# State-space rounds: 32-row matmuls for the decays and the head spread, and a skip term written by ScalarE

## The reference, cut to what matters

```
dt    = softplus(dt_raw + dt_bias)             # one per token, head and direction
y_fwd = ssd_chunked(x * dt_f, dt_f * A[0], B, C)
y_bwd = flip(ssd_chunked(flip(x * dt_b), flip(dt_b * A[1]), flip(B), flip(C)))
y     = y_fwd + y_bwd + ssd_D[:, None] * x     # the last is the skip term
ssd   = rms_norm(y * silu(z), ssd_norm_w)
# inside a chunk of 128 tokens, per head:
M[l, s] = (C[l] . B[s]) * exp(cs[l] - cs[s])  for s <= l    # cs: cumulative sum of dt * A
```

## Time and profile before

| | |
|---|---|
| median of 3 runs | 925.79 us |
| the three runs | 925.61, 925.79, 929.63 us |
| the profiled execution | 920.72 us |
| its span | 918.9 us |
| TensorE busy (page) | 894.4 us, 97% of the span |
| VectorE, ScalarE, GpSimd busy | 668.6, 512.5 and 79.0 us |
| mean granted TensorE clock | 0.994 |

### The profile page before, as it was taken

How to read it: one execution, slowest core, us unless ns; L and a number is a source line. 1 busy time by engine, 2 the same in 40 slices (tenths; PEclk the granted TensorE clock), 3 DMA queues, 4 the chain that set the end, 5 groups by cost and what they waited for, 6 DMA issues and landing times.

```text
span 918.9 us, 18092 instructions
## 1 busy us (share of the span) xinstructions
PE 894.4 (97%) x7444; PEld 851.2 (93%) x7444; DVE 668.6 (73%) x918; ACT 512.5 (56%) x696; POOL 79.0 (9%) x56
## 2 busy tenths in 40 slices
PE   5999999999999999999999999999998999999998
PEld 3899998888888889999999999988998999999998
DVE  6877998998699988777866545545886766666642
ACT  2566756577878774335555543446567654554431
POOL 0133000000455440000000000000000000000000
PEclk9999999999999999997999999999999999999999
DMA  9764553757322237483755655544431345555660
GB/s 377 305 244 147 198 190 121 280 217 251 116 90 93 92 131 260 184 302 118 283 191 183 206 206 184 183 155 167 139 138 47 138 144 200 206 184 183 231 205 23
DMA packets 25084, 168.00 MB, mean 183 GB/s; under 512 B 2868, under 2 KB 4532, under 8 KB 5048
## 3 DMA queue, kind: packets, MB, share of 16 engines
q1 hardware_dynamic: 23760, 164.90, 50.7%
q10 hardware_dynamic: 1256, 2.12, 0.7%
HBM read 165.95 MB, written 1.06 MB: 182 GB/s over the span
## 4 chain that ended last, share of the span: by engine, by line
PE 75%; DVE 10%; ACT 7%; DMA 4%; issue 3%; SPq 0%; DVEq 0%; ACTq 0%
PE bank L1864 74%; DVE wlo L1107 3%; ACT whi L573 3%; DMA raw<-w_stream 2%; DVE acc L1152 1%; DMA adas<-w_stream 1%; DVE cvt L1341 1%; ACT kw__113 L822 1%; PE bank L2137 1%; DVE eb L1432 1%; ACT ew L789 0%; DVE p L1319 0%; ACT prob L724 0%; PE bank L2161 0%; DVE kw__113 L1441 0%
## 5 line engine op out<-in xcount | busy, mean ns | idle before, releaser
L1864 PE MATMUL bank<-hhi,whi 128*128 128x256 f32 (+1 forms) x1364 | 382.8, 283 | 0.9 <-DVE hlo L1210 0.6
L1864 PE MATMUL bank<-hlo,whi 128*128 128x256 f32 (+1 forms) x1352 | 375.4, 278 | 0.0
L1864 PE MATMUL bank<-hhi,wlo 128*128 128x256 f32 (+1 forms) x1352 | 373.7, 278 | 0.0
L1107 DVE TENSOR_TENSOR wlo<-raw,whi 128x2048 fp32r<-128x2048 f32 (+1 forms) x130 | 298.9, 2300 | 101.0 <-ACT whi L573 98.9
L573 ACT ACTIVATE whi<-raw 128x2048 fp32r<-128x2048 f32 (+1 forms) x132 | 250.9, 1901 | 97.2 <-PE bank L1864 71.9
L1864 PEld LDWEIGHTS bank<-hhi,whi 128*128 128x128 f32 (+1 forms) x1364 | 256.0, 188 | 10.8 <-issue 9.9
L1864 PEld LDWEIGHTS bank<-hlo,whi 128*128 128x128 f32 (+1 forms) x1352 | 255.4, 189 | 0.2
L1864 PEld LDWEIGHTS bank<-hhi,wlo 128*128 128x128 f32 (+1 forms) x1352 | 253.7, 188 | 0.0
L1864 PE MATMUL bank<-fhi,whi 128*128 128x256 f32 x432 | 119.2, 276 | 0.0
L1864 PE MATMUL bank<-flo,whi 128*128 128x256 f32 x432 | 119.2, 276 | 0.0
L1864 PE MATMUL bank<-fhi,wlo 128*128 128x256 f32 x432 | 119.2, 276 | 0.0
(11 more groups left out here) (298 smaller groups left out, 1320.1 us busy)
## 6 DMA issues: line engine op xcount, KB each, us to landing
raw<-w_stream SPq DMA_DIRECT2D x147, 1024.0 KB, 4.9
adas<-w_stream SPq DMA_DIRECT2D x8, 1024.0 KB, 8.7
xres<-x_t SPq DMA_DIRECT2D x1, 1024.0 KB, 10.2
out<-oute SPq DMA_DIRECT2D x8, 128.0 KB, 4.1
tabs<-tabs_in_dram ACTq DMA_DIRECT2D x1, 641.0 KB, 8.7
tabs<-tabs_in_dram ACTq DMA_DIRECT2D x1, 512.0 KB, 3.6
hankel<-bucket_rows ACTq DMA_DIRECT2D x1, 512.0 KB, 10.8
cols<-cols_in_dram ACTq DMA_DIRECT2D x1, 325.0 KB, 8.2
```

Source lines behind the costliest of these rows:

```text
L1107: nc.vector.tensor_tensor(out=wlo[:, c % RING, 0:n], in0=raw[:, r % RING, 0:n], in1=whi[:, c % RING, 0:n].bitcast(f32), op=ALU.subtract)\
L1864: return nc.tensor.matmul(out, lhsT, rhs, start=start, stop=stop)
```

## The change

- The cumulative sums are kept for each head, direction and chunk in 32 rows per group (`dtax`, four roles of 8 heads). `row_roles` on GpSimd turns them into two tensors: `css`, stationary, and `csr`, from which `own_rows` makes `bd`. A decay is then one matmul over 32 rows, with both terms of the difference in it.
- The head spread is one matmul over 32 rows, with `par` stationary and `pairs_` moving; `pairs_` is a sum made on GpSimd (`pair_rows`), once for each chunk. `group_halves`, `grp`, `gsel`, `ngsel` and `ind` go.
- `skipped` on GpSimd and the identity matmul go. `bank_opened` opens `side[5]` with a matmul whose product isn't used, ahead of `products`, and ScalarE's `iteration_skip` then writes the skip term into the same bank in four pieces, between its split and `iteration_parts`. `outputs_own` waits for it.
- The two masked products are one instruction (`cb2`).
- The new tensors lie in `xres`, so x is loaded again, on ScalarE's queue behind the rounds, and `tabs2` is loaded there too. VectorE waits for it ahead of `wo`.

```diff
+            def row_roles():
+                nc.gpsimd.tensor_scalar(css[:, :, :], csr[:, :, :].bitcast(f32), marks[:, 0, 1:2], marks[:, 1, 0:1],
+                                        ALU.mult, ALU.add).then_inc(csr_done, 1)
+                pool.wait_ge(csr_done, 3)
+                nc.gpsimd.tensor_scalar(csr[:, :, :], csr[:, :, :].bitcast(f32), marks[:, 0, 0:1], marks[:, 0, 1:2],
+                                        ALU.mult, ALU.add).then_inc(csr_done, 1)
+            def pair_rows(t):
+                d = 1 - t
+                own = bd[:, d * HG:(d + 1) * HG, :].bitcast(f32).rearrange("p (j two) l -> p two j l", two=2)
+                if t == 1:
+                    pool.wait_ge(bc_done, NG)
+                pool.wait_ge(bd_done, 2 + 2 * t)
+                nc.gpsimd.tensor_tensor(out=pairs_[:, :, :], in0=own[:, 0], in1=own[:, 1], op=ALU.add)\
+                  .then_inc(bd_done, 1)
...
             pool.wait_ge(dec_done, 1)
-            pool.wait_ge(csr_done, 6)
-            pool.wait_ge(sel_done, 5)
+            pool.wait_ge(csr_done, 2)
+            pool.wait_ge(sel_done, 6)
+            row_roles()
...
             own_rows(0, 1)
+            pair_rows(0)
             for i in range(8):
-                group_halves(i)
...
                 decayed(i)
-                if i < NG:
-                    skipped(i)
                 if i >= 2:
                     weighted(i - 2)
                     if i == NG - 1:
                         pool.wait_ge(segf_done, NG)
                         own_rows(1, 0)
+                        pair_rows(1)
                     squares(i - 2)
...
+            def iteration_skip(i):
+                g, t = i % NG, i // NG
+                act.wait_ge(open_done, i + 1)
+                for j in range(4):
+                    nc.scalar.activation(side[5][:, j * P:(j + 1) * P], xcv[:, 4 * g + j, t * P:(t + 1) * P], ACT.Copy,
+                                         scale=col("ssdd", 4 * g + j)).then_inc(skip_done, 1)
...
                 if k > 1:
                     split(c + AHEAD)
+                if 2 <= k <= 9:
+                    iteration_skip(k - 2)
                 if 3 <= k <= 10:
                     iteration_parts(k - 3)
...
+                if k == 11:
+                    act.wait_ge(yd_done, 8)
+                    act.dma_start(tabs2[:, :], tabs2_dram).then_inc(tabs2_in, 16)
+                    act.dma_start(xres[:, :, :], x_dram).then_inc(x_in, 16)
...
+                    dve.wait_ge(dta_done, 1)
+                    nc.vector.tensor_copy(
+                        dtax[:, :, :].rearrange("p a (g r j) -> p (a g) r j", g=NG, r=4),
+                        spread(dta[:, :, :].rearrange("p t (x j) -> p (t x) j", j=HG), 2, 4)).then_inc(dta_done, 1)
...
-                for dst, mask in ((cbf, "le"), (cbb, "ge")):
-                    nc.vector.tensor_tensor(out=dst[:, :], in0=side[2][:, 0:P], in1=tab(mask),
-                                            op=ALU.mult).then_inc(cbm_done, 1)
+                masks = tabs[:, TSPAN["le"][0]:TSPAN["ge"][1]].rearrange("p (a l) -> p a l", a=2)
+                nc.vector.tensor_tensor(out=cb2[:, :, :], in0=spread(side[2][:, 0:P], 1, 2), in1=masks,
+                                        op=ALU.mult).then_inc(cbm_done, 1)
...
-                for part in range(2):
-                    own = bd[:, (1 - t) * HG:(2 - t) * HG, :].rearrange("p (j two) l -> p two j l", two=2)[:, part]
-                    last = mm(side[4][:, :], grp[:, i % 2, HD - part * HD:HD - part * HD + P], own, part == 0, part == 1)
-                last.then_inc(bc_done, 1)
+                rows = slice(g * 4 * HG, (g + 1) * 4 * HG)
+                mm(side[4][:, :], par[rows, :], pairs_[rows, :, :]).then_inc(bc_done, 1)
...
+                rows = slice(g * 4 * HG, (g + 1) * 4 * HG)
                 for k in range(2):
-                    heads = d * NH + g * HG + 4 * k
-                    mm(side[k][:, :], group(g, P), bd[:, d * HG + 4 * k:d * HG + 4 * k + 4, :], True, False)
-                    last = mm(side[k][:, :], csr[:, t, :], spread(ind[:, heads:heads + 4], 2, P), False, True)
+                    last = mm(side[k][:, :], css[rows, 2 * t + d, :], bd[rows, d * HG + 4 * k:d * HG + 4 * k + 4, :])
...
-            def outputs_own(i):
-
-                g, t = i % NG, i // NG
+            def bank_opened(i, c, moving):
+
                 if i == 0:
                     pe.wait_ge(mod_done, 3)
                 else:
                     pe.wait_ge(ydr_done, i)
+                mm(side[5][:, :], whi[:, c % RING, 0:P], moving[:, 0:2, :], True, False).then_inc(open_done, 1)
...
+                pe.wait_ge(skip_done, 4 * (i + 1))
                 pe.wait_ge(w_done, i + 1)
-                pe.wait_ge(skip_done, g + 1)
-                mm(side[5][:, :], tab("ident"), xcv[:, 4 * g:4 * g + 4, t * P:(t + 1) * P], True, False)
```

More of the change, by code:

```diff
@@ L117, in transformer_pair @@
     hlo = place("hlo", [P, KD, T], f32r)
+    xres0 = here[0]
     xres = place("xres", [P, KD, T], f32)
@@ L126, in transformer_pair @@
     dec = place("dec", [P, NT, NH], f32)
-    rq0 = here[0]
     rq = place("rq", [P, NT, 20], f32)
     rqs = place("rqs", [P, NT, 20], f32)
-    grp = place("grp", [P, 2, 3 * HD], f32r)
-    gsel = place("gsel", [P, NG], f32)
-    ngsel = place("ngsel", [P, NG], f32r)
+    par = place("par", [P, P], f32r)
+    cb2 = place("cb2", [P, 2, P], f32)
+    dsel = place("dsel", [P, HG], f32)
+    marks = place("marks", [P, 4, 2], f32)
     acc = place("acc", [P, 2, 512], f32)
@@ L135, in transformer_pair @@
     eb = place("eb", [P, 2 * 512], f32, A0 - 4 * KB)
[L136 to L138 removed]
+    csr = place("csr", [P, 2 * NT, P], f32r, xres0)
+    css = place("css", [P, 2 * NT, P], f32r, xres0 + 2 * KB)
+    dtax = place("dtax", [P, 2 * NT, P], f32, xres0 + 2 * KB)
+    pairs_ = place("pairs_", [P, HG // 2, P], f32r, xres0 + 4 * KB)
     qt = place("qt", [P, KD, T], f32, A0)
@@ L477, in decayed @@
                                         in1=spread(w, 2, HD), op=ALU.mult).then_inc(xd_done, 1)
-            def skipped(g):
-                x = xcv[:, 4 * g:4 * g + 4, :]
-                nc.gpsimd.tensor_tensor(out=x, in0=x, in1=spread(col("ssdd", 4 * g, 4), 2, T), op=ALU.mult)\
-                  .then_inc(skip_done, 1)
             def weighted(i):
@@ L705, in _ @@
                     act.wait_ge(cst_done, 1)
-                    for part in range(2):
-                        for d in range(2):
-                            rows = slice(part * 2 * NH + d * NH, part * 2 * NH + (d + 1) * NH)
-                            nc.scalar.activation(csr[rows, :, :], side[3][rows, :].rearrange(
-                                "p (t d l) -> p t d l", t=NT, d=2)[:, :, d, :], ACT.Copy).then_inc(csr_done, 1)
+                    nc.scalar.activation(csr[:, :, :].rearrange("p a l -> p (a l)"), side[3][:, :], ACT.Copy)\
+                      .then_inc(csr_done, 1)
                 if i >= 1:
@@ L1348, in _ @@
                 if i == 11:
-                    dve.wait_ge(csr_done, 4)
-                    for d in range(2):
-                        rows = slice(2 * NH + d * NH, 2 * NH + (d + 1) * NH)
-                        nc.vector.tensor_tensor(out=csr[rows, :, :], in0=side[3][rows, :].rearrange(
-                            "p (t d l) -> p t d l", t=NT, d=2)[:, :, d, :], in1=csr[rows, :, :].bitcast(f32),
-                            op=ALU.subtract).then_inc(csr_done, 1)
+                    dve.wait_ge(csr_done, 1)
+                    dve.wait_ge(sel_done, 6)
+                    rows = csr[:, :, :].rearrange("p a l -> p (a l)")
+                    nc.vector.scalar_tensor_tensor(out=rows, in0=rows.bitcast(f32), scalar=marks[:, 2, 1:2],
+                                                   in1=side[3][:, :], op0=ALU.mult, op1=ALU.add).then_inc(csr_done, 1)
                     dve.wait_ge(dexp_done, 1)
@@ L1540, in _ @@
             dve.wait_ge(mod_done, 3)
+            dve.wait_ge(x_in, 32)
             for i in range(4):
@@ L2093, in _ @@
                     mm(side[5][:, NH:2 * NH], tab("lt"), dta[:, 1, NH:2 * NH]).then_inc(dsum_done, 1)
-                    masks = tabs[:, TSPAN["le"][0]:TSPAN["ge"][1]]
                     for t in range(NT):
-                        for part in range(2):
-                            last = mm(side[3][part * 2 * NH:(part + 1) * 2 * NH, t * 2 * P:(t + 1) * 2 * P],
-                                      dta[:, t, :], masks)
+                        for d, mask in ((0, "le"), (1, "ge")):
+                            last = mm(side[3][:, (2 * t + d) * P:(2 * t + d + 1) * P], dtax[:, 2 * t + d, :],
+                                      tab(mask))
                     last.then_inc(cst_done, 1)
```

75 lines of the change are left out of this document (31 added, 44 removed).

## The result

| | before | after |
|---|---|---|
| median on the same chip | 925.61 us (5 runs) | 931.83 us (5 runs, 930.19 to 934.39) |
| ratio | | 1.0066, 95% interval 1.0041 to 1.0092 |
| profiled execution, its span | 920.72, 918.9 us | 930.19, 928.4 us |

The change costs 6.2 us. The same kernel measured again on another chip gave 1.0112 (1.0071 to 1.0153).

What follows compares the result with a forecast made beforehand. VectorE, taking turns with GpSimd on SBUF, was taken to bound the steps, TensorE being full too. Terms -1.3 + 2.1 + 0 + 0.4 = +1.2 us gave 927.0 us, range 918.5 to 933, no measurable change at 0.50.

Steps and rivals of the forecast that it cites:

- the end of the rounds: Last own outputs up to `so`: they begin 0.95 earlier, but TensorE then waits longer for `rcol`, so 0.
- Ahead of the rounds: Cumulative sums and subtraction gain 0.2 each, `row_roles` covering the `smax` product costs 0.8; sum +0.4 us.
- steps 1 and 2: First two steps, where VectorE waits for TensorE: fewer matmuls gain 0.8 and 0.5, together -1.3 us, bounds -0.5 and -2.0.
- Step 3: No `tat` product, but a longer head loop: 11.7 us for 11.85, -0.15.
- Steps 4 and 5: `pair_rows(1)` queues between `own_rows` and `sqs` on GpSimd: +1.0 us, bounds -1.0 and +3.0.
- Steps 6, 7, 8: GpSimd's later `sqs` and `xd` take turns from VectorE: 12.4, 12.4 and 11.9 us, or +0.35, +0.5 and +0.4.
- the fast rival: `sqs` and `xd` run beside `eb` in VectorE's free stretch, steps fall to 10.9: 918.5 us; chance 0.21.
- The reload of x: 1 MB load on ScalarE's queue, competing with the weight stream: 0 on the path, up to 4.9 us without reserve chunks.
- The 32-row form: 32-row matmuls stream like others; changes of array shape cost 0.3 us a round, bounds 0 and 0.6.
- The turns and step 5 cost their full length: Each GpSimd operation costs VectorE its whole 1.04 us; steps 6 to 8 at 13.0, 13.0, 12.0: 932 us; chance 0.16.
- The clock falls: TensorE's idle time in the steps drops its granted clock, +2 us for each occurrence: 934 us; chance 0.08.
- Signs: TensorE 80 to 85% busy in steps 3 to 8; wrong if steps 6 to 8 under 11.2, TensorE stays busy, clock drops.

Runs made afterwards that it cites:

- skip_alone: The kernel before with only the skip part: ScalarE's four pieces and `bank_opened` in place of `skipped` and the identity matmul; ratio 1.0050 to the kernel before.
- skip_last_early: The changed kernel with round 7's skip pieces written ahead of ScalarE's split in step 9, not behind it; ratio 1.0076 to the kernel before.
- skip_behind_ew: The changed kernel with skip pieces of rounds 0 to 6 behind the `ew` copies, round 7's ahead of step 9's split; ratio 1.0021 to the kernel before.
- rows32_alone: The changed kernel without the skip part (`skipped` and the identity matmul as before); ratio 1.0041 to the kernel before.
- rows128: The changed kernel with decays and spread over all 128 rows instead of their group's 32; one run, no ratio, steps 4 and 5 27.83 us.
- combo2: The changed kernel with skip pieces behind `ew`, second-chunk rows behind `squares(1)` and `sslo`, `rcol` ahead of a split, x reload behind the root; 1.0004 to before.

## Why the prediction was right, and where not

The time, 931.83, lies in the range, 4.8 us above the forecast. I gave 0.50 to a change within 0.5%; the ratio is 0.66%, just outside, with an interval that reaches down to 0.41%. The change is slower by more than 0.5%, to which I gave 0.24; the second measurement, 1.0112, says so with its whole interval. The forecast of the rounds' steps was right in its sum by luck and wrong in its parts; the step that failed is the end of the rounds.

- **Ahead of the rounds, steps 1 and 2:** forecast +0.4 and -1.3. The second `smax` product after `row_roles` took 0.17 us, so the 0.8 for it did not come. The start is 241.3 on average over the ten profiles with the new early work and 242.4 over the four without, each spread over 3 to 4. The spread is in part the pace from 100 to 140 us; among profiles of one pace the difference of the means is 1.3 (242.0 and 243.3 at 118 ns, 240.3 and 241.5 at 113), so some -1, by few profiles. Step 2 is 0.17 shorter, not 0.5.
- **Step 3:** 11.7 forecast, 11.15 measured.
- **Steps 4 and 5:** +1.0 forecast, +2.9 measured (+3.2 again), at the upper bound. The mechanism was named, the size was not: I put one operation's length on `pair_rows` behind `own_rows` and took the place from the old trace, beside one long product. TensorE being ahead released `own_rows` 5 us into the step, not 6, into eight short operations.
- **Steps 6, 7, 8:** 12.4, 12.4 and 11.9 forecast; 12.03, 11.36 and 12.03 measured. In step 7 `xd` ran beside the bank reads (311.65 to 313.14), as the fast rival had it, and in step 8, where none follows, `sqs` cost `sslo` 1.07. Steps 3 to 8 come to +2.2 (75.08 for 72.86) against +2.1: steps forecast 2.0 too long and 2.1 too short cancel.
- **The end of the rounds:** "The last own outputs begin 0.95 earlier without the identity matmul" and "0". Their head matmuls began 10.3 us behind the last `eb`, before 8.6, and the stretch grew by 4.6 and 3.7. I priced the four pieces in an ordinary step, and did not ask about the one with two table loads, where ScalarE is last; nor that the late `Square` that I had worked out for `sqs` makes the exponential late, and with it those loads. Shown by skip_alone (+3.5), skip_last_early (-1.8) and skip_behind_ew (-4.8).
- **The reload of x:** 0 forecast, 0 shown. **The 32-row form:** 0.3 a round estimated, 0.26 in the part that was compared.
- **Rivals.** "The turns and step 5 cost their full length", 932 us, has the number and in steps 4 and 5 the mechanism, but its steps of 13.0 did not come. "The clock falls" came true in two places. In steps 4 and 5 it cost little, if rows32_alone is the measure (28.51 against 28.32 at full clock); in step 9 the slower own outputs (0.9) and 14 matmuls at 213 ns (1.3) cost 2.2 us, by the rows.
- **Signs.** One of those that I named for being wrong came, the clock's fall inside the rounds. TensorE was busy 93% of steps 3 to 8 (before 99%), not 80 to 85. Steps 6 to 8 averaged 11.8, neither under 11.2 nor from 12.9.
- **Open.** The rest took 265.8 us on average over the four profiles without the new 32-row part and 267.8 over nine with it (rows128 left out, which ran a long part of it at 118 ns), mostly in the waits behind `wo` (1.0 and 2.6 us on average). It is not the reload. The traces show the late link: the first `xres` sum stands behind ScalarE's split of a chunk, and that split starts when the chunk has landed. ScalarE, before and after:

```profile
395.53 1.92 ACT L573 ACTIVATE whi<-raw 128x2048 fp32r<-128x2048 f32 x1 [0.19 <-DMA raw<-w_stream]
...
400.30 1.92 ACT L577 ACTIVATE whi<-raw 128x2048 fp32r<-128x2048 f32 x1 [0.96 <-DMA raw<-w_stream]
```

It starts 1.5 to 2.3 us behind the first `wo` matmul in the four profiles and 2.5 to 4.2 in the ten with the 32-row part. In three of the ten (rows32_alone, skip_last_early, combo2) the chunk was asked for 1 to 2 us later; in the other seven it took 5.5 to 6.9 us to land, not 4.8 to 5.1. Why, no run here shows.

## What to carry to other kernels

Price a moved operation in the step where its new engine is latest, not in the typical one: here the skip pieces of seven rounds cost 0.7 us over steps 3 to 8 (skip_alone), and those of the eighth 3 to 4 us. Ask of an operation on GpSimd not only how long it is but whether it will meet one long VectorE operation or the seams of many short ones, and remember that a faster engine upstream moves it. And compare profiles between two events of the same stretch before explaining a difference of whole spans.

## What the runs showed that was not expected

- TensorE's stream of 256-column matmuls runs at one of two paces with the granted clock at 1.00 in both: 113 or 118 ns from start to start. An execution keeps one through a long stretch (1,490 matmuls, 168.7 or 176.2 us) and can have the other elsewhere. This is enough for differences of 7 us between two executions of one kernel.
- Issuing the 1 MB load on ScalarE's queue directly behind another held the engine's queue for 0.45 to 2.25 us in nine profiles (2.25 and 1.29 in the two of the changed kernel), and 0.33 or 0.34 in the two where the issue ahead of it lay further back; it did not show in the time.
- Waits of TensorE of 3.5 us in step 9 were followed each time (six profiles) by a granted clock of 0.5; one of 2.34 as well, for fewer matmuls; those of 1.05 in three profiles were not. The length of one wait doesn't settle it: in skip_alone the clock fell at 286.6, about a wait of 1.64 us, and behind `wo` it fell about waits of 0.62 to 2.10 but not about 0.27.
